# Weight blocks loaded in four pieces two products apart, and one group of transposes in another PSUM bank, in a two-layer hybrid encoder trunk

## The reference, cut to what matters

```python
for l in range(DEPTH):                       # 2 layers; x is 1024 tokens x 1024
    h = _rmsnorm(x, norm_g[l])
    p = h @ w_in[l]                          # 1024 x 8904
    pa, pb, pc, pd, dz, pg = split(p)        # columns of four mixers, and four gates of 1024
    oa = chunk_band_attention(...) * silu(az)        # A: 5-tile key band
    ob = hgrn2(...) * silu(bz)                       # B
    oc = dsa(...) * silu(cz)                         # C: top-256 keys by an indexer, then softmax
    od = rwkv7(...) * silu(dz)                       # D
    y = sigmoid(ga)*(oa@wb0) + sigmoid(gb)*(ob@wb1) + sigmoid(gc)*(oc@wb2) + sigmoid(gd)*(od@wb3)
    x = x + y @ w_out[l]
return _rmsnorm(x, final_g)
```

## Time and profile before

| what | value |
|---|---|
| median of three runs | 2764.34 us (2760.86 to 2766.89) |
| profiled execution, its own time | 2762.82 us |
| its span, first to last instruction | 2761.0 us |
| TensorE busy | 2716.2 us, 98% |
| VectorE, ScalarE, POOL busy | 58%, 35%, 29% |
| granted TensorE clock | 0.999 |

### The profile page before, as it was taken

The page is one execution under the profiler, slowest core; times in us unless marked ns, Lnnn a source line. Parts: engine busy times, 40 slices in busy tenths (PEclk is TensorE's granted clock), DMA queues, the critical chain, the costliest instruction groups (busy, mean ns, idle before and its releaser), DMA issues.

```text
span 2761.0 us, 46225 instructions
## 1 busy us (share of the span) xinstructions
PE 2716.2 (98%) x18624; PEld 1465.9 (53%) x18624; DVE 1595.5 (58%) x3018; ACT 973.2 (35%) x1869; POOL 802.5 (29%) x582
## 2 busy tenths in 40 slices
PE   8999999999999999999999999999999999999999
PEld 4447444466574565544444464544665745755443
DVE  4689876754508732265337898767545178232753
ACT  3455665321224224500124556643112332344001
POOL 3333312411334332133033333124113443321420
PEclk9999999999999999999999999999999999999999
DMA  4221111211111223183142121112111112232731
GB/s 163 68 59 50 46 35 53 70 45 45 47 42 39 63 82 102 32 281 116 41 123 57 46 62 39 36 49 71 50 37 47 46 43 66 70 107 79 246 111 46
DMA packets 135612, 200.90 MB, mean 73 GB/s; under 512 B 8392, under 2 KB 90472, under 8 KB 134632
## 3 DMA queue, kind: packets, MB, share of 16 engines
q1 hardware_dynamic: 116808, 163.86, 19.8%
q10 hardware_dynamic: 18592, 34.09, 3.3%
HBM read 146.53 MB, written 44.59 MB: 69 GB/s over the span
## 4 chain that ended last, share of the span: by engine, by line
PE 44%; DVE 4%; ACT 1%; issue 1%; POOL 0%; DVEq 0%; ACTq 0%
PE ps L498 23%; PE ps L495 4%; PE ps L757 4%; PE ps L771 3%; PE ps L1163 1%; PE ps L1152 1%; PE ps L1498 1%; PE ps L1176 1%; DVE arena L1898 1%; DVE arena L1640 1%; PE ps L2018 1%; PE ps L2112 1%; PE ps L2010 0%; DVE arena L1624 0%; PE ps L1964 0%
## 5 line engine op out<-in xcount | busy, mean ns | idle before, releaser
L498 PE MATMUL ps<-hT,wr 128*128 128x512 f32 x1856 | 858.9, 600 | 3.1 <-PEq L2574 2.8
L498 PEld LDWEIGHTS ps<-hT,wr 128*128 128x128 f32 x1856 | 338.7, 191 | 375.6 <-issue 367.1
L498 PE MATMUL ps<-sums,wr 128*128 128x512 f32 x928 | 438.4, 600 | 1.1 <-ACT gts L568 0.7
L673 POOL TENSOR_TENSOR gts<-gts,wr 128x512 f32<-128x512 f32 x96 | 153.7, 1601 | 621.0 <-ACT wr L549 400.7
L1252 DVE CUSTOM_DVE_ANT_0 arena<-ps,arena 128x640 f32<-128x640 f32 (+7 forms) x128 | 90.5, 707 | 334.1 <-PE ps L1152 317.4
L498 PEld LDWEIGHTS ps<-sums,wr 128*128 128x128 f32 x928 | 167.2, 190 | 180.9 <-issue 171.6
L549 ACT ACTIVATE wr<-ps 128x512 f32<-128x512 f32 x174 | 103.2, 593 | 369.7 <-PE ps L498 324.2
L757 PE MATMUL ps<-xo,arena 128*128 128x512 f32 x512 | 220.1, 592 | 0.0
L498 PE MATMUL ps<-wr 128*128 128x512 f32 x464 | 218.5, 600 | 0.0
L1640 DVE TENSOR_SCALAR_CACHE_REDUCE arena<-arena,sm 128x384 f32<-128x384 uint16 (+7 forms) x256 | 192.8, 809 | 2.2
L642 POOL TENSOR_TENSOR wr<-wr 128x512 f32<-128x512 f32 x57 | 81.2, 1425 | 382.9 <-PE ps L498 347.7
(11 more groups left out here) (321 smaller groups left out, 4139.2 us busy)
## 6 DMA issues: line engine op xcount, KB each, us to landing
wr<-in_w_in SPq DMA_DIRECT2D x36, 1024.0 KB, 5.5
gate_tanh<-gts ACTq DMA_DIRECT2D x128, 256.0 KB, 3.3
arena<-gate_tanh SPq DMA_DIRECT2D x128, 256.0 KB, 2.9
wr<-in_w_in SPq DMA_DIRECT2D x104, 256.0 KB, 2.8
wr<-in_w_in SPq DMA_DIRECT2D x16, 512.0 KB, 3.8
arena<-in_w_branch SPq DMA_DIRECT2D x8, 1024.0 KB, 7.7
wr<-in_w_out SPq DMA_DIRECT2D x8, 1024.0 KB, 7.4
arena<-arena SPq DMA_DIRECT2D x36, 128.0 KB, 2.6
```

The costliest lines, as they stand in the source:

```text
L498: ins = pe.matmul(ap, lhsT=right(u, w_side)[:, kt, :], rhs=left(h_side, kt), start=fresh and kt == 0, stop=kt == half_k - 1, skip_group_ch ...
L673: pool.tensor_tensor(dst, dst, stage_of(u), ALU.add).then_inc(sg("pool_added"), 1)
```

## The change

In `load_parts` the condition changes: in four pieces is now loaded the first (or only) block of every unit from the third on, if the unit before it is a single. These are 27 blocks of a layer in place of 13. Whole remain C0, D1, A0 and gate 13. A pair's first block is among the 27. The pieces after the first are issued at products 0, 2 and 4 of the unit in between, where they were issued at 0, 1 and 2. In `turn` the second group of the last step (u = 31) of each attention goes to the bank S2[0].

```diff
             def load_parts(n):
 
                 u = next(u for u in range(len(units)) if n in units[u][1])
-                return 4 if units[u][0] == "gate" and units[u - 1][0] == "gate" else 1
+                return 4 if u >= 2 and n == units[u][1][0] and len(units[u - 1][1]) == 1 else 1
...
                     quarter = KT // 4
                     for q in range(4):
-                        key = done if q == 0 else (*fill_done[n - 1][0][:3], q - 1)
+                        key = done if q == 0 else (*fill_done[n - 1][0][:3], 2 * q - 2)
                         k0 = quarter * q
                         loads.append((key, wr[:, 2 + n % 2, k0:k0 + quarter, 0:w], c0, w, sg(f"fill_w_loaded{n % 2}"), sums_of, k0))
...
                     g, n = group
                     key = ("PT", b, u, g)
-                    ap = jobs.open(pe, key, T)
+                    ap = jobs.open(pe, key, S2[0] if g and u + 1 == len(units) else T)
```

## The result

The changed kernel takes 2787.45 us (median of 4 runs, 2784.37 to 2788.14), the kernel before 2765.61 (4 runs). The ratio is 1.008, 95% interval 1.0062 to 1.0097: slower by 22 us, where 15 us were forecast (2779 against the 2764 shown then).

A forecast was written before the change was run, and what follows sets the result against it. TensorE's own instruction stream was taken as the bound, busy 2716.2 of 2761.0 us. Stalls of 8.3 us a layer, twice 16.6, on the profiled 2762.8 gave 2779.4, predicted as 2779; range 2762 to 2790.

The forecast's parts named there:

- The chain: From product 4's end: last piece, t1, add, ScalarE's take-out of product 5; 6.1 us behind a projection, 7.0 behind a gate.
- hidden: Rival: the chain fits its room everywhere, so the change is not slower, 2762 to 2769 us; chance 0.16.
- The room of 6.7 us: Where fills are dense, the time from product 4's end until TensorE needs product 5's bank for the next unit: 6.7 us.
- gates 3 and 9: Dense ends, gate 3 to 4 and gate 9 to 10: chain late, stall 0.4 us each, 0.8 a layer.
- the projections' ends A0, A3 and C0: Unit ends behind a projection: the chain just fits, with 0.6 us of room, so no stall.
- gate 5: Gate 5 to 6: VectorE's long instructions hold POOL's t1; stall 1.8 us a layer, bounds 0.3 and 2.4.
- B0: B0 to B3: t1 and the add take 3.31 us each beside VectorE; stall 3.6 us, bounds 0 and 4.1.
- the pair: Pairs' first blocks: t1 comes after the add, perhaps 0.8 us later; 0.2 us for three, bounds 0 and 1.5.
- Gate 10: Gate 10 to 11, mixer B: t1 held in the add's place, add 1.3 us later; 0.9 us, bounds 0 and 1.5.
- Attention: Gates 0 and 13: late adds delay ScalarE, then TensorE's transposes; 0.3 and 0.7, together 1.0 us, bounds 0 and 2.0.
- the search as cover: Top-k search: ScalarE held some 0.7 us at three unit ends, costed at nothing because VectorE waited 8.8 us afterwards; otherwise 2.
- third rival: Whole 1024 KB loads slow a gate's store or a needed copy; spreading them gains, 2756 us at best; chance 0.04.

The follow-up runs named there:

- 2: Changed kernel with the pieces after the first issued at products 0, 1 and 2 again: 2760.18 us, ratio 0.9986.
- 8: Changed kernel with the pieces after the first issued at products 0, 2 and 3: 2761.89 us, ratio 0.9996.
- 3: Changed kernel with POOL making t1 of the next unit after the add of product 4, not before it: 2767.87 us, ratio 1.0016.
- 11: Kernel before with C5's block alone in pieces, issued at products 0, 2 and 4: 2766.57 us, ratio 1.0008.
- 7: Kernel before with POOL making t1 after the add of product 4, loads as before: 2771.78 us, ratio 1.0032.
- 5: Changed kernel with the blocks of the layer's first part (C1, D4, C4, C5, first of pair C2+3) loaded whole again: 2785.04 us.
- experiment 9: Kernel before with B0's block also in pieces, at products 0, 1 and 2, and no turn: 2760.72 us, ratio 0.9988.
- experiment 6: Kernel before with its 13 gate blocks in pieces issued at products 0, 2 and 4, nothing else changed: 2777.03 us, ratio 1.0053.

## Why the prediction was right, and where not

**The chain: right.** That the last piece at product 4 holds t1, t1 the add, the add ScalarE and ScalarE TensorE is shown by three edits, each of which cuts one link: the piece comes earlier (2 and 8), or the add goes first (3). The rivals of the prediction fall with them: it was not hidden, and the number of transfers cost nothing (2).

**The room of 6.7 us: right.** At gates 3 and 9 the stalls are 0.3 and 0.4 against 0.4; the projections' ends A0, A3 and C0 with 0.6 of room show none, as forecast. At gate 5 it is 1.4 against 1.8, at B0 3.6 against 3.6, for the pair 0.3 against 0.2.

**Gate 10: wrong, 0 against 0.9.** "Now t1 is held in its place and the add comes after it, 1.3 later" failed: POOL came in between VectorE's short instructions, 1.56 for t1 and 1.71 for the add, and was done as early as the one held add of 3.89 in the earlier trace rows.

**Attention: too small, 3.2 against 1.0.** Gate 13 was right (0.9 against 0.7), gate 0 twice what I took (0.7), and gate 1, which I had let pass because its chain fits, cost 1.5. There POOL's later work ran beside VectorE's selection of keys (L652 took 2.99 and L673 2.21), and scores and transposes came late. That this is the cause is argued from the timeline, not tested by itself.

These terms sum to 9.2 in the first layer, against 8.3 in the sum of the prediction.

**The step that failed inside it: the search as cover.** "I cost this at nothing for VectorE, since it waited 8.8 us for TensorE's first scores afterwards" looked at the search's end. The loss is at its start. POOL's late sums stand beside L1627, which takes 9 instead of 4.9 us; the first bits come late; and ScalarE's take-outs are put into its stream behind its work on those bits (L1547), so TensorE, which is ahead by a fixed count of fills, finds the bank full. That is 2.0 a layer, shown by 11 (the one late block makes it) and by 3 and 7 (it comes with early pieces too, if POOL's order is late). The index stage lost 1.6 a layer at L1498, where VectorE's L1613 ran beside POOL's late sums (1.50 us against 0.62 for the 128x384 one); 5 takes this away, and half of it (0.85) comes in 3 and 7 too. Together 3.6 in each layer.

**What the sum did not have at all: the clock.** I added idle time only. The kernel before has two short stretches at half clock, 1.7 us lost at each: from 660 to 665 (the lines of experiment 9), and between the layers:

```profile
1394.00:1399.00 5.00, 4.15 (x6) 1.88 (x7) 4.08 (x4) 0.00 (x0) 0.00 (x0) 0.66 0.68 227
```

The changed kernel has neither but pays 3.4 behind B0 and 1.7 behind C5 in the second layer, 1.7 more in all.

**What it did not have either: a gain.** Its third rival had a load in the way of a store or a copy, not of TensorE, and gave it 0.04. "Nothing in TensorE's waits names a transfer" is true, and misled, because the longest single wait behind the start names nothing. It stands in the kernel before, and the earlier trace rows passes over it:

```profile
PE ps L2010 <- issue: 4.4, 2, 3.0
```

Experiment 9 shows that the 3.0 us hang on B0's whole block. In pieces it is worth 3.5 us (0.8 to 6 by the interval).

The account of the profiled execution: first layer 9.2 + 3.6 - 4.3 and some 0.6 of small shifts, 9.1; between the layers -1.7; second layer 8.8 + 3.6 + 5.1 at half clock, less small shifts back, 17.3. Together 24.7 of the 24.8.

**How much of it was luck.** The places that the sum priced took 18.0 (9.2 and 8.8) where it had 16.6, so the forecast of the mechanism stands, though gate 10's 0.9 too much and attention's 2.2 too little cancel in part within it. What it did not price was a loss of 7.2 at the search and the index stage and 1.7 of clock, and against them 2.6 of wait gained at gate 7. That these cancelled in part, and left the time 2.5 us under the top of the range, was not foreseen. The forecast of 2779 is also 1.5 lower than its own sum: 16.6 was added to the profiled execution's 2762.8, and the result was held against the median.

## What to carry to other kernels

Before a transfer is moved later, find the engine that waits for it and read what stands behind the waiting instruction in that engine's stream; the room is counted there, to the bank that comes free last, and not to the data's first use. Waits that "cost nothing" (POOL's 516 us) turn into a full loss one step later, and a POOL that works later meets VectorE at other instructions, so that the cost can lie far from the edit, as at the start of the search. A wait that ends on nothing named still has a cause: here it was worth 3.0 us. Of the versions run, 27 blocks in pieces at products 0, 1 and 2 (2760.2 us) is the fastest, by 0.14% over the kernel before, and experiment 9 has nearly all of that gain (3.5 of 3.9) with one block.

## What the runs showed of the hardware

A wait of 3.35 us on TensorE was followed by nothing in one layer and by half clock worth 3.4 us in the other, at the same instructions; from kernel to kernel such stretches change their place, and in the profiles of this study they cost between 1.7 and 8.5 us in all, the last microseconds of the program left out (each of them 1.7 or 3.4). Behind the wait of 3 us in mixer D the half clock came in five of six profiles (not in experiment 6). What decides stays open.

A whole block of 1024 KB, on its way while TensorE worked through many 64x64 products, went with a wait of 2.8 to 3.1 us on TensorE, and took 7.0 us to land instead of 5.5; in four pieces neither was seen. The page of the profile lists two DMA queues of kind "instruction", and the traces tell more of the path. In all 13 profiles the L2010 instruction that ends this wait starts 1.27 to 1.50 us after the end of one 16 KB packet on such a queue (q8). With B0's block whole this packet ends 3.1 to 3.3 us after the start of the two L498 records ahead of it, with the block in pieces 0.3 to 0.6. The other waits over 0.25 us on "issue" at L2010, L2112, L2166, L1742 and L2155, in the kernels before and after, end 1.25 to 1.5 us after such a packet as well. So by these times TensorE's instructions came late, behind the block's packets; no run moved the instruction packet alone. In the second layer the whole block of B0 had no such wait behind it.

VectorE and POOL: the Trainium skill, "SBUF — State Buffer", section "SBUF: two separate sides", has the loser wait for the whole instruction. At B0 the runs agree (3.25 and 3.30 for 1.27). By the same rule whichever starts first has the pair. A run of VectorE's short instructions (0.68 each) at gate 10 let POOL in once (1.56) and had held it once through several of them (3.89); what decides between the two is not shown.
